# Order of the first projection's products, a second layout of the modulation vector through DRAM, and two z tiles ahead of retention

## What is computed

```
mod = silu(c) @ w_ada + b_ada                     # 6 * 1024 numbers
shift1, scale1, gate1, shift2, scale2, gate2 = split(mod, 6)
h = rmsnorm(x, norm1_w) * (1 + scale1) + shift1   # 1024 x 1024
proj = h @ w_in                                   # r_q r_k r_v r_g | d_q d_k d_v d_z | d_a d_b
rq, rk = rotary(r_q, positions), rotary(r_k, positions)
ret = rmsnorm(retention(rq, rk, r_v)) * silu(r_g) # 8 chunks of 128 tokens, 4 heads
... delta rule on the d_ columns, w_out, residual with gate1 ...
h2 = modulate(rmsnorm(x, norm2_w), shift2, scale2)
... mixture of experts on h2, residual with gate2, then the second block ...
```

## Time and profile before

| what | us |
|---|---|
| median of 3 runs | 3127.25 |
| lowest and highest run | 3123.01, 3130.77 |
| the profiled execution's own time | 3127.57 |
| its span in the profile | 3125.8 |
| end of `front` on PE, start of the barrier | 265.9 |
| first matmul of `delta_conv` | 383.69 |

### The profile page before, as it was taken

How to read it: one execution, slowest core, us unless ns; L and a number is a source line. 1 busy time by engine, 2 the same in 40 slices (tenths; PEclk the granted TensorE clock), 3 DMA queues, 4 the chain that set the end, 5 groups by cost and what they waited for, 6 DMA issues and landing times.

```text
span 3125.8 us, 30644 instructions
## 1 busy us (share of the span) xinstructions
PE 2902.0 (93%) x11996; PEld 1728.9 (55%) x11996; DVE 1176.3 (38%) x1997; ACT 628.1 (20%) x1348; POOL 680.8 (22%) x528
## 2 busy tenths in 40 slices
PE   6998999798893999989959999999999999999998
PEld 5886544688642766666634445557644444444443
DVE  6614444566314111111134134569824424123143
ACT  4001232232221122112222131137421000000001
POOL 3213343554221000000021000127612221202221
PEclk9999999899995999999979999999999999999999
DMA  7724298000314999999862000030211101111101
GB/s 260 236 34 44 38 229 189 1 28 1 110 68 184 405 424 426 427 425 427 362 229 81 35 26 14 14 105 1 75 41 54 41 27 54 40 54 40 41 27 54
DMA packets 177591, 419.81 MB, mean 134 GB/s; under 512 B 26964, under 2 KB 100116, under 8 KB 168344
## 3 DMA queue, kind: packets, MB, share of 16 engines
q1 hardware_dynamic: 165769, 375.22, 34.4%
q0 software_dynamic: 5904, 21.50, 1.8%
q10 hardware_dynamic: 5760, 20.97, 1.7%
HBM read 366.03 MB, written 59.87 MB: 136 GB/s over the span
## 4 chain that ended last, share of the span: by engine, by line
PE 86%; DVE 5%; DMA 4%; issue 2%; ACT 2%; POOL 1%; SPq 1%; POOLq 0%; ACTq 0%; DVEq 0%
PE bank L3494 27%; PE bank L2272 8%; PE bank L2275 7%; PE bank L2691 5%; PE bank L1047 5%; PE bank L714 4%; PE bank L1714 4%; PE bank L2861 3%; PE bank L232 3%; PE bank L2859 2%; PE bank L3193 2%; PE bank L3203 2%; PE bank L840 2%; PE bank L1617 1%; DMA wa_rest<-in_w_ada 1%
## 5 line engine op out<-in xcount | busy, mean ns | idle before, releaser
L3494 PE MATMUL bank<-w_ff,uT 128*128 128x512 f32 x640 | 276.0, 592 | 0.0
L3494 PE MATMUL bank<-hT,w_ff 128*128 128x512 f32 x512 | 224.2, 596 | 4.3 <-DVE hT L3297 4.3
L3494 PEld LDWEIGHTS bank<-w_ff,uT 128*128 128x128 f32 x640 | 121.6, 190 | 153.0 <-issue 153.0
L3617 DVE TENSOR_TENSOR x_out<-x_out,bank 128x512 f32<-128x512 f32 x140 | 94.5, 685 | 291.7 <-PE bank L3494 291.5
L2272 PE MATMUL bank<-e_w,e_xsT 128*128 128x256 f32 x832 | 185.5, 384 | 1.7 <-DVE e_xsT L2357 1.6
L2275 PE MATMUL bank<-e_w,e_xsT 128*64 128x256 f32 x1408 | 162.0, 391 | 21.7 <-issue 21.7
L2272 PEld LDWEIGHTS bank<-e_w,e_xsT 128*128 128x128 f32 x832 | 158.7, 192 | 33.3 <-issue 11.3
L1047 PE MATMUL bank<-hT,w_qkv 128*128 128x512 f32 x384 | 167.3, 593 | 2.2 <-DMA w_qkv<-in_w_in 1.4
L2691 PE MATMUL bank<-w_gla,nT 128*128 128x512 f32 x384 | 167.9, 598 | 1.3 <-ACT nT L2655 1.3
L3494 PEld LDWEIGHTS bank<-hT,w_ff 128*128 128x128 f32 x512 | 97.6, 191 | 126.2 <-issue 125.9
L3494 PE MATMUL bank<-h_sum,w_ff 128*128 128x512 f32 x384 | 166.1, 592 | 0.0
(11 more groups left out here) (517 smaller groups left out, 4835.4 us busy)
## 6 DMA issues: line engine op xcount, KB each, us to landing
e_w<-in_w SPq DMA_DIRECT2D x105, 2048.0 KB, 30.4
w_ff<-in_w_ff SPq DMA_DIRECT2D x32, 1024.0 KB, 5.2
y_rows<-zero SPq DMA_DIRECT2D x8, 3008.0 KB, 17.5
wa_rest<-in_w_ada SPq DMA_DIRECT2D x32, 512.0 KB, 5.3
y_rows<-e_y ACTq DMA_DIRECT2D x24, 512.0 KB, 9.6
wa<-in_w_ada SPq DMA_DIRECT2D x16, 512.0 KB, 10.5
w_in<-in_w_in SPq DMA_DIRECT2D x16, 512.0 KB, 9.3
w_qkv<-in_w_in SPq DMA_DIRECT2D x12, 512.0 KB, 9.0
```

The source lines that it names most:

```text
L3494: t = pe.matmul(bank[:, :], still, moving, start=step in (0, 1, 3) and f == 0, stop=f == 3, skip_group_check=True)
L3617: v.tensor_tensor(dst, dst, k.bank[4 * ((ph + step) % 2) + g][:, :], ALU.add).then_inc(*s.added.up().inc)
```

## The change

Six things are changed. (a) The order on PE becomes (0, 0), (1, 0), (0, 1), and so on; the turning of tiles 4 to 7 moves from (1, 0) to (0, 1), `front_columns` of the second half moves ahead of the last piece of (0, 0), and the second half of tile 3 is turned within (1, 0). (b) The token sums are split: DVE makes s1 and s2 with each tile and the other two, for all tiles, after the sums of (0, 1) into `qkvg`; PE waits for them ahead of (0, 4) and (0, 5). (c) The last two early w_ada pieces of half 0 have a semaphore each. (d) The rest products are spread as 8, 4, 8, 12 over (0, 1), (0, 4), (0, 5), (1, 1) instead of 4, 3, 8, 10, 3, 4 up to (1, 5), the loads of w_in blocks take other places among theirs, the rotary angles move from after (1, 5) to after (1, 4) on DVE, and the sines from after (1, 6) to after (1, 3) on ACT. (e) The 16 strided matmuls go; SP writes shift2 and scale2 to a DRAM tensor in feature order (one element at a time) and reads them back in the other layout; DVE makes `affine_rows` after its last sum into `qkvg`, behind a wait for that. (f) In retention two z tiles (16 matmuls) are put ahead of the first round, on PE and ACT, and the rate is 1.6 instead of 2.

```diff
-FRONT_ORDER = [(0, 0), (0, 1), (1, 0)] + [(0, n) for n in range(2, STEPS)] + ...
+FRONT_ORDER = [(0, 0), (1, 0)] + [(0, n) for n in range(1, STEPS)] + ...
...
+def front_early_piece(s, h, n):
+    if h == 0 and n >= NK - 2:
+        return (s.wa_3, s.wa_4)[n - NK + 2], 1
+    return front_early_got(s)[h][n // 2], 2
...
-        for ph, role in {8: ((1, 3),), 11: ((2, 0),), 12: ((2, 1),), 16: ((2, 2),), 30: ((2, 3),)}.get(q, ()):
+        for ph, role in {7: ((1, 3),), 11: ((2, 0),), 15: ((2, 1),), 21: ((2, 2),), 31: ((2, 3),)}.get(q, ()):
             front_w_load(k, s, b, ph, role)
     for role in range(4):
         front_w_load(k, s, b, 3, role)
+    sy.wait_ge(*s.rest_out(1))
+    sy.wait_ge(*s.place_loaded(2))
+    sy.dma_start(mod_rows.rearrange("j (f p) -> p j f", p=P), b.mod[:, 2 * NK:4 * NK].rearrange("p (j f) -> p j f", j=2), allow_slow_non_contiguous=True).then_inc(...)
+    sy.wait_ge(*s.place_loaded(3))
+    sy.dma_start(b.mod[:, 4 * NK:6 * NK].rearrange("p (j n) -> p j n", j=2), mod_rows.rearrange("j (p n) -> p j n", p=P)).then_inc(...)
...
 def front_sums_vector(k, s, b, hT, m):
-    v.tensor_tensor(s1, a21, a22, ALU.add)...
+    v.tensor_tensor(s1, hT[:, 0:4, hi], hT[:, 4:, hi], ALU.add)...
     v.wait_ge(*s.x_summed.now())
-    v.tensor_tensor(s2, s1, a11, ALU.subtract)...
-    v.tensor_tensor(a21, a11, a21, ALU.subtract)...
-    v.wait_ge(*s.x_summed.now())
-    v.tensor_tensor(s4, a12, s2, ALU.subtract)...
+    v.tensor_tensor(s2, s1, hT[:, 0:4, lo], ALU.subtract)...
+def front_sums_late_vector(k, s, b, hT):
+    v.wait_ge(*s.x_summed(8))
+    for m in range(4):
+        v.tensor_tensor(hT[:, 0:4, hi], hT[:, 0:4, lo], hT[:, 0:4, hi], ALU.subtract)...
+    for m in range(4):
+        v.tensor_tensor(b.sums[2][:, :, lo], hT[:, 4:, lo], b.sums[1][:, :, lo], ALU.subtract)...
...
 def front_vector(...):
     for i in range(4):
         front_turned_vector(k, s, hT, affine, i)
-    front_add_vector(k, s, b, 0, 1)
     for i in range(4, NT):
         front_turned_vector(k, s, hT, affine, i)
         front_sums_vector(k, s, b, hT, i - 4)
+    front_add_vector(k, s, b, 0, 1)
+    front_sums_late_vector(k, s, b, hT)
...
-        for _ in range({(0, 1): 4, (0, 4): 3, (0, 5): 8, (1, 1): 10, (1, 4): 3, (1, 5): 4}.get((ph, step), 0)):
+        for _ in range({(0, 1): 8, (0, 4): 4, (0, 5): 8, (1, 1): 12}.get((ph, step), 0)):
...
-            v.tensor_copy(b.mod[:, 2 * NK:6 * NK], k.bank[4][:, 0:4 * NK])...
+            v.tensor_copy(b.mod[:, 2 * NK:4 * NK], k.bank[4][:, 0:2 * NK])...
-            (the two instructions of affine_rows)
-        if (ph, step) == (1, 5):
+        if (ph, step) == (1, 4):
             v.wait_ge(*s.constants_loaded(2))
             rotary_vector(k, s, b)
...
+    v.wait_ge(*s.place_loaded(4))
+    (the two instructions of affine_rows)
...
 def front_scalar(...):
     front_rows_pair_scalar(k, s, b, 6)
+    front_copy_scalar(k, s, b, 1, 0)
...
-        if (ph, step) == (1, 6):
+        if (ph, step) == (1, 3):
             (the two sines)
...
 def front_tensor(...):
         if (ph, step) == (0, 1):
-            front_columns(k, s, b, 1)
             pe.wait_ge(*s.columns_out(2))
+            pe.wait_ge(*s.half_1_out(16))
-        if (ph, step) == (1, 0):
-            front_turn_next(k, s, b, 4)
+        if (ph, step) in ((0, 4), (0, 5)):
+            pe.wait_ge(*s.x_summed(8 + 4 * (step - 3)))
...
             if (ph, step) == (0, 1):
-                pe.wait_ge(*s.half_1_out(4 * (g + 1)))
+                front_turn_next(k, s, b, 4 + g)
             if (ph, step) == (0, 2):
-                pe.wait_ge(*s.x_summed(4 * (g + 1)))
+                pe.wait_ge(*s.x_summed(2 * (g + 1)))
...
+            if (ph, step) == (0, 0) and g == 2:
+                front_columns(k, s, b, 1)
+            if (ph, step) == (1, 0) and g == 1:
+                pe.wait_ge(*s.half_1_out(4))
+                front_turn(k, s, b, 3, 1)
...
 def front_rest(k, s, b, n):
-        for j in range(2 * NK):
-            at = (3 + j // NK) * D + j % NK
-            t = pe.matmul(k.bank[4][:, 2 * NK + j:2 * NK + j + 1], b.acc[:, at:at + D - j % NK:NK], k.c("ones")[:, 0:1], ...)
...
 def retention(...):
+    fill = z_units_scalar(k, s, z)
+    for _ in range(NK * Z_AHEAD):
+        next(fill)
-    weave(rounds(...), z_units_scalar(k, s, z), 2.0)
+    weave(rounds(...), fill, Z_RATE)
+    (the same for the tensor engine's list)
+Z_AHEAD = 2
+Z_RATE = 1.6
```

More of the change, by code:

```diff
@@ L252 @@
 FRONT_PHASES = 4
-FRONT_ORDER = [(0, 0), (0, 1), (1, 0)] + [(0, n) for n in range(2, STEPS)] + [(1, n) for n in range(1, STEPS)] + [(ph, n) for ph in (2, 3) for n in range(STEPS)]
+FRONT_ORDER = [(0, 0), (1, 0)] + [(0, n) for n in range(1, STEPS)] + [(1, n) for n in range(1, STEPS)] + [(ph, n) for ph in (2, 3) for n in range(STEPS)]
 FRONT_PLACES = ((0, 0), (0, 0), (0, 1), (1, 1), (1, 1), (0, 1), (1, 0))
@@ L565, in front_vector @@
                 v.tensor_copy(dst, k.bank[(5, 6, 7, 4)[n]][:, :]).then_inc(*s.rest_out.up().inc)
+    v.wait_ge(*s.place_loaded(4))
+    v.scalar_tensor_tensor(affine_rows[:, 0, :], b.mod[:, 5 * NK:6 * NK], 1.0, cols[:, 4, :], ALU.add, ALU.mult).then_inc(*V.up().inc)
+    v.tensor_copy(affine_rows[:, 1, :], b.mod[:, 4 * NK:5 * NK]).then_inc(*V.up().inc)
     a21, a11 = hT[:, 0:4, BANK:], hT[:, 0:4, 0:BANK]
@@ L628, in front_scalar @@
     front_rows_pair_scalar(k, s, b, 6)
+    front_copy_scalar(k, s, b, 1, 0)
     for i in range(4, NT):
         front_turned_scalar(k, s, hT, affine, i)
-    for ph, step in FRONT_COPIES[1:]:
+    for ph, step in FRONT_COPIES[2:]:
         front_copy_scalar(k, s, b, ph, step)
-        if (ph, step) == (1, 6):
+        if (ph, step) == (1, 3):
             for n, out in enumerate((b.sin, b.cos)):
@@ L716, in front_tensor @@
                 t.then_inc(*s.product_made.up().inc)
-            if (ph, step) == (0, 0):
+            if (ph, step) == (0, 0) and g < 3:
                 front_turn(k, s, b, g, 1)
-            if (ph, step) == (1, 0) and g < 3:
-                front_turn_next(k, s, b, 5 + g)
+            if (ph, step) == (0, 0) and g == 2:
[3 more added lines that the diff above has]
+                front_turn(k, s, b, 3, 1)
         if (ph, step) in ((2, 2), (2, 4)):
@@ L744, in front_rest @@
                 at = j * D + f * P
-                pe.matmul(k.bank[4][:, m * NK + f:m * NK + f + 1], b.acc[:, at:at + P], k.c("ones")[:, 0:1], start=True, stop=True)
-        for j in range(2 * NK):
-            at = (3 + j // NK) * D + j % NK
-            t = pe.matmul(k.bank[4][:, 2 * NK + j:2 * NK + j + 1], b.acc[:, at:at + D - j % NK:NK], k.c("ones")[:, 0:1], start=True, stop=True)
+                t = pe.matmul(k.bank[4][:, m * NK + f:m * NK + f + 1], b.acc[:, at:at + P], k.c("ones")[:, 0:1], start=True, stop=True)
         t.then_inc(*s.rest_made.up().inc)
@@ L816, in retention @@
     two = range(2)
-    weave(rounds(*(retention_scalar(k, s, b, f, retT, n) for n in two)), z_units_scalar(k, s, z), 2.0)
-    weave(rounds(*(retention_tensor_tile(k, s, b, f.qkvg, n) for n in two)), itertools.chain(z_units_tensor(k, s, hT, wz), gates_units_tensor(k, s, hT, conv_s, conv_b)), 2.0)
+    fill = z_units_scalar(k, s, z)
+    for _ in range(NK * Z_AHEAD):
+        next(fill)
+    weave(rounds(*(retention_scalar(k, s, b, f, retT, n) for n in two)), fill, Z_RATE)
+    fill = itertools.chain(z_units_tensor(k, s, hT, wz), gates_units_tensor(k, s, hT, conv_s, conv_b))
+    for _ in range(NK * Z_AHEAD):
+        next(fill)
+    weave(rounds(*(retention_tensor_tile(k, s, b, f.qkvg, n) for n in two)), fill, Z_RATE)
     k.meet(sync=False, behind=True)
@@ L3715, in build @@
         ret_s, wz = retention_signals(k), k.at("w_z", front_at(124), P, NK, BANK)
-        front(k, b, hT, affine, affine_rows, cols, gate2, kept, early, ret_s, wz)
+        front(k, b, hT, affine, affine_rows, cols, gate2, kept, early, dram("mod_rows", 2, D), ret_s, wz)
         conv_s = delta_conv_signals(k)
```

44 lines of the change are left out of this document (23 added, 21 removed).

## The result

The changed kernel takes 3108.23 us (median of 5 runs, 3105.71 to 3114.10) against 3127.90 before (5 runs): ratio 0.9942, interval 0.9927 to 0.9956. The forecast was 3101 with a range of 3092 to 3110. So the sign and the range held, and about a quarter of the expected 26.4 us is missing. The profiled execution is the slowest of the five, 3114.10, and by itself outside the range.

What follows compares the result with a forecast made beforehand. PE, busy 93% of the span, was taken as the bound, so time is won only where it idles, runs at lower clock or sheds work. 5.0 + 14.6 + 6.8 = 26.4 us gave 3101 us, range 3092 to 3110.

Steps and rivals of the forecast that it cites:

- Front's start: Start of front, order and token sums: (0, 2) starts at 64.85 against 69.80, gain 5.0 us, bounds 2.5 to 6.8.
- I take 46: Front's start: (1, 0) starts at 46 us, its w_in block landing between 43.5 and 48.2.
- 1 us for the lower clock: Front's start: 1 us allowed for PE's lower clock, so (0, 1) starts at 54; before it cost 1.84.
- Middle, parts d and e: Middle of front: ACT wait, low clock and strided matmuls go, gain 14.6 us, bounds 12.5 to 16.3.
- 7.61 + 2.2 - 1.75: Middle of front: 7.61 us strided matmuls, 2.2 clock in the gates' spreading, less 1.75 clock lost behind remaining thin matmuls.
- both neighbours' estimate: DRAM round trip: writing 2048 elements takes 15 or 31 us, from two nearest rows, both with pieces over 100 bytes.
- Rate of the rest products: DVE in front: 1.62 us each, sums done 4.5 us before (1, 3) and 4.4 before (1, 6) on PE.
- signs that it is wrong: PE waiting for DVE at (1, 3) or (1, 6), write over 65 us, clock low through (2, 3), or longer later stage.
- the rest products are late: Rival, front: products of 2 us or more beside POOL's sums make PE wait ahead of (1, 6); 3105 to 3109, chance 0.14.
- Retention: From front's end to delta_conv: waits and slow clock of 9.4 us go, some given back; gain 6.8 us, bounds 5 to 9.
- I take 2: Retention's last pass: 2 us given back for lacking z filler over the transposes and copies, out of 0 to 3.4.
- The slower rival: Rival, DRAM round trip: the single-element write delays PE's first z product, deciding from 65 us on; about 3140, chance 0.03.

Runs made afterwards that it cites:

- e0: The changed kernel run again with nothing altered, for a second trace; ratio 0.9932 to the kernel before.
- e1: Changed kernel with the three w_in blocks for phase 2 that stood among the rest loads loaded behind the last of them; ratio 0.9908 to the kernel before.
- e2: Changed kernel with SP loading the w_in block for (1, 0) ahead of the two others of phase 0; ratio 0.9925 to the kernel before.
- e3: Changed kernel with rest products spread 8, 4, 4, 8, 4, 4 up to (1, 5), angles and sines moved into phase 3; ratio 0.9906 to the kernel before.
- e5: Changed kernel with retention's part undone: no z tiles ahead of the first round, rate 2; ratio 0.9957 to the kernel before.
- e8: Changed kernel with phase 2's w_in blocks behind the last rest load and (1, 3)'s behind the fourth; ratio 0.9912 to the kernel before.

## Why the prediction was right in sign, and where it was short

*Front's start (5.0 forecast, 2.5 in the first trace, 4.7 in e0).* DVE's share of a tile fell as worked out: turns follow each other by 2.8 us, and the gap ahead of the last turn is gone. What was mis-sized is the step "I take 46" with "1 us for the lower clock": (1, 0) started at 47.4 and lost 1.8 us of clock. Over all traces with the new order (0, 2) starts at 64.1 to 69.4, a gain of 0.4 to 5.7, which the bounds of 2.5 to 6.8 do not hold.

*Middle, parts d and e (14.6 forecast).* The 4.75 us wait for ACT and the 1.76 of clock behind it went, in every trace with the changed front. Part e was right in size: from the first thin matmul to (2, 3) it is 9.1, 7.6, 7.9, 6.1, 7.8, 6.2 and 7.9 us (first trace, e0, e1, e2, e3, e5, e8), 7.5 on average, against 15.8: 8.2 won, where 7.61 + 2.2 - 1.75 = 8.1 was forecast. The round trip was hidden and shorter than both neighbours' estimate: 11.4 us to landing for 2048 elements, 5.6 ns each, where 15 to 31 was bounded. The Trainium skill ("DMA: Bandwidth & Descriptors", Rules for kernel authors) says one descriptor per element; the trace agrees, with 2336 more packets under 512 bytes on the page (29300 against 26964), where the write's 2048 elements and the read's 256 pieces make 2304. The "some 15 us of transfer" for w_z were read from the wrong row: the 15.3 us in the earlier trace rows are a later load of 128 KB. The 2 MB load landed in 12.6 us in the changed kernel, so nothing came of it.

The step that failed is in part d: "Rate of the rest products ... 1.62 us each ... Both are hidden, narrowly". By it twelve products, eight and four, would end near 93, and the sums of (1, 1) at 108.7. They started at 118.64. 3.6 us of this are the late start (76.88 for 73.3). The first eight took 1.6 us each, but the four behind (0, 4) took 3.0 each, 5.6 us more than at the forecast rate; the next eight took 1.8 and the last twelve 1.95. DVE waited 12.8 us for loads (six times; 11.6 to 14.1 in the others of that order). PE's own need was only 2.6 us later than forecast (115.8 for 113.2), so the 4.5 us of cover did not do. PE waited at (1, 3) and at (1, 6), which the prediction itself had named as signs that it is wrong: 5.5 us of waits and 1.76 of clock.

The rate had been taken from a stretch in which one block of w_in was landing. The trace of the kernel before has the other kind too, in its timeline of DVE:

```profile
98.30 2.48 DVE L485 SCALAR_TENSOR_TENSOR mod_acc<-wa_rest,cT,mod_acc 128x1024 f32<-128x1024 f32 x2
103.55 2.20 DVE L485 SCALAR_TENSOR_TENSOR mod_acc<-wa_rest,cT,mod_acc 128x1024 f32<-128x1024 f32 x1 [2.77 <-DMA wa_rest<-in_w_ada]
...
114.59 2.67 DVE L485 SCALAR_TENSOR_TENSOR mod_acc<-wa_rest,cT,mod_acc 128x1024 f32<-128x1024 f32 x2 [2.77 <-DMA wa_rest<-in_w_ada]
```

From 98.30 to 117.18, with four blocks of w_in issued from 93.14 to 112.27, eight products took 2.36 us each. From the first rest product to the last sums behind them, less the sums, the 32 products take 1.96 us each in the first trace, 1.75 in e1 and 1.69 in e8, where no block is left among the reloads: close to the 1.62. So what the rate left out is the blocks that stand between the rest loads. e3 shows the cost by taking the sums out from behind the rest products (7.9 us come back), e8 by clearing the loads.

The rival *the rest products are late* came true at the place it named, at 3105 to 3109 with a chance of 0.14 (the median is 3108.2), but in the main not for its reason. It had the products themselves slowed beside POOL's sums. That is there, some 11 us over all 32 (an estimate: the rows of line 498 add up to 50.1 us, where starts 1.2 us apart give 39), but the 1.62 had its share of it: ten products take 15.3 us in that stretch, 3 more than at 1.2. What it did not have is the waits: 1.0 us for ten there, 12.8 for 32 here.

*Retention (6.8 forecast, 9.2 found).* The mechanism was right, the term "I take 2" was too dear. In the last pass the transposes have no filler, and the row at 349.06 is 2.33 us instead of 1.95: 0.4 us for all of it. The 0.2 us a pass do not show: 20 records (8.6 us) cover the chain of DVE.

*The sum.* For front the forecast was 19.6, found 7.6 in the first trace and 11.3 in e0, with the late loads and the waits behind them; 9.2 for 6.8 in retention made up a part. That the median lies in the range is in part luck: without these 2.4 us it would be 3110.6, outside. No trace shows a cost behind `delta_conv`, as assumed. The slower rival was far off: its mechanism would have needed 65 us, and the write took 10.4 to 14.0 in the ten traces with it.

*What stays open.* Whether the clock falls behind the plain thin matmuls differs between traces that have the same order there (2.82 us in e2 and e5, 4.34 to 5.47 in five others), and three traces with them spread are too few to call that settled. The same holds for the clock at the start of (1, 0). Why the first products of `delta_conv` to the output projection take between 432 and 440 us was not tried. The separate semaphore for the early pieces (part c) was not tried alone; DVE took the last four pieces without a pause and then waited 6.37 us for PE, so nothing speaks for a gain.

## What to carry to other kernels

A wait that is taken away on one engine brings the next-late queue to light: here DVE's work was packed before sums that PE needs, in order to free a later place, and the packing cost 7 us of what the freed place gave. Put work with a far due time behind the sums with a near one, even if its loads then wait longer: e3 had more DMA waits than the change and was 8 us better. A rate that is read from a stretch holds only for that stretch's company of loads (1.62 us a product in one, 2.36 in the other, in the same trace); where the cover is 10% of the work that hides, count the slots, the loads put between and the chance of the start being late, and take the rival for a case of its own.
